# Places of a gathered expert's tokens: spread over the partitions by a matmul out of a resident table, in place of a broadcast transfer

## The reference

```python
scores = jax.nn.sigmoid(xf @ w_router)
_, idx = lax.top_k(jnp.where(expert_mask, biased, NEG_INF_2), TOP_K)
w = jnp.take_along_axis(scores, idx, axis=-1)
w = w / (jnp.sum(w, axis=-1, keepdims=True) + 1e-20) * ROUTED_SCALE
...
out = swiglu_2(xpad[toks], w1[e], w3[e], w2[e])        # for each block of one expert's tokens
return out * wts[:, None].astype(out.dtype)
...
routed = jax.ops.segment_sum(y.reshape(n_slots, D), slot_tok, num_segments=T + 1)[:T]
shared = swiglu_2(xf, ws1, ws3, ws2)
```

## Time and profile before

| | |
|---|---|
| median of three runs | 3819.14 us (3814.4 to 3822.09) |
| the profiled execution | 3815.19 us |
| its span | 3813.2 us, mean granted clock 0.964 |
| TensorE busy | 3526.2 us, 92% |
| VectorE, ScalarE busy | 2335.9 us (61%), 1474.9 us (39%) |
| DMA | 842.63 MB, mean 221 GB/s |
| chain that ended last | TensorE 76%, DMA 10%, VectorE 9%, ScalarE 3% |

### The profile page before, as it was taken

How to read it: one execution, slowest core, us unless ns; L and a number is a source line. 1 busy time by engine, 2 the same in 40 slices (tenths; PEclk the granted TensorE clock), 3 DMA queues, 4 the chain that set the end, 5 groups by cost and what they waited for, 6 DMA issues and landing times.

```text
span 3813.2 us, 52585 instructions
## 1 busy us (share of the span) xinstructions
PE 3526.2 (92%) x21065; PEld 2984.2 (78%) x21065; DVE 2335.9 (61%) x3513; ACT 1474.9 (39%) x2212; POOL 242.0 (6%) x337
## 2 busy tenths in 40 slices
PE   4998899998899997899999999999989999999999
PEld 2997799997699886689777777778878976666676
DVE  6774376775377465446666666656644766666666
ACT  1432234432143203223555555541232355555554
POOL 3010000010001001000000000000000000000000
PEclk9998899998899998889999999999988999999999
DMA  7785176695068645236889998875522688898886
GB/s 250 253 294 191 58 259 223 212 311 177 28 229 302 216 138 192 73 98 214 272 274 297 289 299 283 271 244 193 166 77 83 217 277 270 285 290 278 285 277 193
DMA packets 580320, 842.63 MB, mean 221 GB/s; under 512 B 22715, under 2 KB 489760, under 8 KB 578832
## 3 DMA queue, kind: packets, MB, share of 16 engines
q1 hardware_dynamic: 514508, 665.85, 53.3%
q0 software_dynamic: 41056, 147.35, 11.7%
q10 hardware_dynamic: 24548, 26.57, 2.8%
HBM read 836.37 MB, written 3.33 MB: 220 GB/s over the span
## 4 chain that ended last, share of the span: by engine, by line
PE 76%; DMA 10%; DVE 9%; ACT 3%; issue 2%; SPq 1%; DVEq 0%; POOL 0%; ACTq 0%
PE bank L987 13%; PE bank L892 11%; PE bank L893 11%; PE bank L894 11%; PE bank L1332 8%; DMA ring<-in_w 3%; DMA far_up<-in_w 3%; DMA wmod<-in_w_mod 3%; PE bank L1199 2%; PE bank L1345 2%; PE bank L1302 2%; PE bank L1303 2%; PE bank L1297 2%; PE bank L1299 1%; PE bank L1298 1%
## 5 line engine op out<-in xcount | busy, mean ns | idle before, releaser
L894 PE MATMUL bank<-hh,ring_lo 128*128 128x256 f32 (+1 forms) x2176 | 620.5, 285 | 0.0
L892 PE MATMUL bank<-hh,hi 128*128 128x256 f32 (+1 forms) x1984 | 570.2, 287 | 16.0 <-issue 12.3
L893 PE MATMUL bank<-h_lo,hi 128*128 128x256 f32 (+1 forms) x1984 | 566.4, 286 | 0.0
L987 PE MATMUL bank<-h,ring 128*128 128x256 f32 x2432 | 553.5, 388 | 8.4 <-ACT h L1509 8.4
L987 PEld LDWEIGHTS bank<-h,ring 128*128 128x128 f32 x2432 | 474.8, 196 | 79.5 <-issue 11.8
L894 PEld LDWEIGHTS bank<-hh,ring_lo 128*128 128x128 f32 (+1 forms) x2176 | 418.6, 192 | 0.0
L892 PEld LDWEIGHTS bank<-hh,hi 128*128 128x128 f32 (+1 forms) x1984 | 382.1, 193 | 24.6 <-issue 17.6
L893 PEld LDWEIGHTS bank<-h_lo,hi 128*128 128x128 f32 (+1 forms) x1984 | 382.2, 193 | 0.5 <-issue 0.5
L892 PE MATMUL bank<-hid,hi 128*128 128x256 f32 (+1 forms) x1216 | 348.1, 286 | 0.0
L893 PE MATMUL bank<-hid_lo,hi 128*128 128x256 f32 (+1 forms) x1216 | 345.4, 284 | 0.0
L894 PE MATMUL bank<-hid,ring_lo 128*128 128x256 f32 (+1 forms) x1088 | 308.9, 284 | 0.0
(11 more groups left out here) (372 smaller groups left out, 6615.1 us busy)
## 6 DMA issues: line engine op xcount, KB each, us to landing
ring<-in_w SPq DMA_DIRECT2D x258, 1024.0 KB, 12.7
ring<-in_ffn_w SPq DMA_DIRECT2D x120, 1024.0 KB, 10.6
wmod<-in_w_mod POOLq DMA_DIRECT2D x216, 512.0 KB, 5.6
far_up<-in_w SPq DMA_DIRECT2D x84, 1024.0 KB, 11.8
ring<-in_w_in SPq DMA_DIRECT2D x74, 1024.0 KB, 6.3
work<-in_w SPq DMA_DIRECT2D x42, 1024.0 KB
ring<-in_w_out SPq DMA_DIRECT2D x16, 1024.0 KB, 5.1
ring<-in_w_mod SPq DMA_DIRECT2D x12, 1024.0 KB, 16.5
```

The source lines that it names most:

```text
L892: pe.matmul(o, w_hi, x_hi, start=start, stop=False, skip_group_check=True)
L893: pe.matmul(o, w_hi, x_lo, start=False, stop=False, skip_group_check=True)
L894: return pe.matmul(o, w_lo, x_hi, start=False, stop=stop, skip_group_check=True)
L987: ins = pe.matmul(o[:, half * T:(half + 1) * T], l_, r_, start=(k == 0), stop=(k == KD - 1))
```

## The change

The table of places stays in SBUF (`place_rows`, 64 partitions by 256 tokens, over `pT`), in the rounded type. For each gathered unit one matmul is put behind `turn_few`: its weights are column `rank` of a 64 by 64 unit matrix (`rank_row`), repeated 128 times, so that the product is row `rank` of the table in all 128 partitions, in the free half of bank 1. `few_turned` now counts this matmul. `spread_slots` reads bank 1 in place of the buffers and waits for `few_turned`; ScalarE's `turned_few` waits for `spread_done` as well, and so do TensorE's `turn_few` and the second up projection of a dense unit behind a gathered one, since they write the bank. The table in HBM, its store, the 98 loads and their semaphores go.

```diff
--- before.py
+++ after.py
@@ -104,7 +104,6 @@
     return WIDE if ORDER[n][0] == "wide" else NARROW
 
 
-RANKS = [r for k, r in ORDER if k in ("wide", "narrow")]
 GATHER_NO = {n: sum(k in ("wide", "narrow") for k, _ in ORDER[:n]) for n in range(len(ORDER) + 1)}
 
 
@@ -358,7 +357,8 @@
         product = nc.alloc_sbuf_tensor_at("product", [P, T], F32, offset=place["macc"] + 4 * (2 * D + 3 * T))
         picks = rounded("picks", [P, 4, 4, P], "wmod")
         spread = rounded("spread", [P, 2, T], "axial")
-        places = [work[:, 65, :], std[:, :]]
+        place_rows = rounded("place_rows", [P, T], "pT")
+        rank_row = rounded("rank_row", [P, N_EXPERTS], "work", 65 * T)
 
         glu = tiles(16, CT)
         ya, yc = tiles(0, 4), tiles(20, 4)
@@ -397,7 +397,6 @@
 
         window_dram = nc.dram_tensor("window_scratch", [NQ, 512], F32, kind="Internal")
         gates_dram = nc.dram_tensor("gates_scratch", [DEPTH, N_EXPERTS, T], F32, kind="Internal")
-        places_dram = nc.dram_tensor("places_scratch", [DEPTH, N_EXPERTS, T], F32, kind="Internal")
         rows_dram = [nc.dram_tensor(f"rows_scratch{l}", [1 + T, D], F32, kind="Internal") for l in range(DEPTH)]
 
 
@@ -421,10 +420,9 @@
             sem(n) for n in ("consts_in", "vecs_in", "x_in", "filter_in", "masks_in", "router_in", "gates_out",
                              "window_out", "bias_in"))
         gates_in = [sem(f"gates_in{v}") for v in range(2)]
-        places_in = [sem(f"places_in{v}") for v in range(2)]
         got_in = [sem(f"got_in{v}") for v in range(2)]
-        sort_in, zero_row_in, rows_in, places_out, kz_cleared = (
-            sem(n) for n in ("sort_in", "zero_row_in", "rows_in", "places_out", "kz_cleared"))
+        sort_in, zero_row_in, rows_in, kz_cleared = (
+            sem(n) for n in ("sort_in", "zero_row_in", "rows_in", "kz_cleared"))
         order_ready = sem("order_ready")
         turned_in, hg_hi_done, hg_done = sem("turned_in"), sem("hg_hi_done"), sem("hg_done")
         pre_done, product_done, few_turned = sem("pre_done"), sem("product_done"), sem("few_turned")
@@ -1305,6 +1303,10 @@
 
                 def turn_few(n):
                     p, wide = GATHER_NO[n], ORDER[n][0] == "wide"
+                    if p == 0:
+                        pe.wait_ge(*X("copied", 1))
+                    else:
+                        pe.wait_ge(spread_done, g0 + p)
                     if wide:
                         pe.wait_ge(product_done, g0 + p + 1)
                         for c in range(2):
@@ -1313,7 +1315,10 @@
                         pe.wait_ge(pre_done, g0 + p + 1)
                         for c in range(4):
                             ins = pe.matmul(bank[1][:, c * NARROW:(c + 1) * NARROW], pre[:, c * P:(c + 1) * P], fold, start=True, stop=True)
-                    ins.then_inc(few_turned, 1)
+
+                    rank = ORDER[n][1]
+                    pe.matmul(bank[1][:, T:2 * T], rank_row[0:N_EXPERTS, rank:rank + 1].to_broadcast([N_EXPERTS, P]), place_rows[0:N_EXPERTS, :],
+                              start=True, stop=True).then_inc(few_turned, 1)
 
                 def finish(n, last=False):
                     if not gathers(n):
@@ -1393,6 +1398,8 @@
                             scatter(n - 2)
                         finish(n - 1)
                         sum_slots(X, LISTED.get((n, 0), ()))
+                        if gathers(n - 1):
+                            pe.wait_ge(spread_done, g0 + GATHER_NO[n])
                         up_dense(n, 1)
                         sum_slots(X, LISTED.get((n, 1), ()))
                         turn_rows(n, GATHER_NO[n])
@@ -1773,9 +1780,6 @@
                 def load_gates(rank):
                     act.dma_start(gates[:, rank % 2, :], gates_dram.ap()[l][rank:rank + 1, :].partition_broadcast(P)).then_inc(gates_in[rank % 2], 16)
 
-                def load_places(p):
-                    act.dma_start(places[p % 2], places_dram.ap()[l][RANKS[p]:RANKS[p] + 1, :].partition_broadcast(P)).then_inc(places_in[p % 2], 16)
-
                 def columns_hi(n):
                     if not gathers(n):
                         return
@@ -1810,6 +1814,7 @@
                         act.activation(pre[:, :], bank[0][:, :], ACT.Copy).then_inc(pre_done, 1)
 
                 def turned_few(n):
+                    act.wait_ge(spread_done, g0 + GATHER_NO[n] + 1)
                     act.wait_ge(few_turned, g0 + GATHER_NO[n] + 1)
                     if slots(n) == WIDE:
                         act.activation(hidden_few[:, :], bank[1][:, 0:T], ACT.Copy).then_inc(hid_done, 2)
@@ -1834,9 +1839,6 @@
                         split_ups(n + 1, 1)
                         out_hi(n - 1)
                         turned_few(n)
-                        if 1 <= GATHER_NO[n] < GATHERED - 1:
-                            act.wait_ge(spread_done, g0 + GATHER_NO[n])
-                            load_places(GATHER_NO[n] + 1)
                     else:
                         rank = ORDER[n][1]
                         if 1 <= rank < WIDE_FROM - 1:
@@ -1850,14 +1852,8 @@
                         silu_dense(n, 1)
                         columns_hi(n + 1)
                         split_ups(n + 1, 1)
-                        if n == 2:
-                            act.wait_ge(*X("copied", 1))
-                            act.dma_start(places_dram.ap()[l], pT_flat[0:N_EXPERTS, 0:T]).then_inc(places_out, 16)
                         if n == 3:
-                            act.wait_ge(places_out, 16 * (l + 1))
                             act.wait_ge(rows_in, 16 * TB * (l + 1))
-                            load_places(0)
-                            load_places(1)
 
             setup_loads()
             load_router(0)
@@ -2523,7 +2519,8 @@
 
             def copy_places(X):
                 dve.wait_ge(*X("turned", 1))
-                dve.tensor_copy(pT_flat[0:N_EXPERTS, 0:T], bank[2][0:N_EXPERTS, 0:T]).then_inc(X["copied"], 1)
+                then(dve.tensor_copy(rank_row[0:N_EXPERTS, :], M["ident"][0:N_EXPERTS, 0:N_EXPERTS]))
+                dve.tensor_copy(place_rows[0:N_EXPERTS, :], bank[2][0:N_EXPERTS, 0:T]).then_inc(X["copied"], 1)
 
             def pick_slots(X, batches):
                 for i in batches:
@@ -2607,10 +2604,10 @@
                 def spread_slots(n):
 
                     p = GATHER_NO[n]
-                    dve.wait_ge(places_in[p % 2], nth(l, p, GATHERED))
+                    dve.wait_ge(few_turned, g0 + p + 1)
                     if g0 + p >= 2:
                         dve.wait_ge(scattered, g0 + p - 1)
-                    dve.tensor_scalar(spread[:, p % 2, :], places[p % 2], own if slots(n) == WIDE else own_few, None, ALU.is_equal).then_inc(spread_done, 1)
+                    dve.tensor_scalar(spread[:, p % 2, :], bank[1][:, T:2 * T], own if slots(n) == WIDE else own_few, None, ALU.is_equal).then_inc(spread_done, 1)
 
                 rank_experts(X)
                 hidden_dense(0, 0)
```

## The result

| | before | after |
|---|---|---|
| median of 20 runs each | 3822.14 us | 3827.52 us |
| ratio, 95% interval | | 1.0019 (1.001 to 1.0028) |
| span of the profiled execution | 3813.2 us | 3826.1 us |
| the two expert layers (first gathered up projection to last down projection, by the timelines) | 709.5 + 721.2 us | 719.6 + 717.9 us |
| TensorE's waits at the down projection | 49.0 us in 34 | 27.6 us in 32 |

I had forecast 3812.7 us. By the ratio the change costs 7 us, and the two expert layers of the profiles show it: +6.8 us. The other 6 us between the spans lie outside of them, where the change touches only the making of the table. What lies outside of the layers took 2379 to 2390 us in the fourteen profiles of this document (before 2382, after 2389), whatever the edit.

What follows compares the result with a forecast made beforehand. TensorE was taken to set the pace, with DMA costing time only through its idle gaps. The terms +11.8 - 2.2 + 7.7 - 3.9 - 19.8 = -6.4 us gave 3812.7 us from the median 3819.14, range 3801 to 3829.

Steps and rivals of the forecast that it cites:

- the new matmul (11.8 - 2.2): TensorE, 98 gathered units: 0.12 us each, 11.8 us, less 2.2 us free in 18 units behind dense ones.
- chain in 14 wide-narrow places: Wide unit, then narrow, then another gathered: spread behind the turn makes the columns 0.55 us late, 7.7 us in all.
- waits for late weights, absorption included: TensorE's varying waits at the down projection: 19.8 us gained, and 3.9 us of added costs absorbed in what is left.
- I stay at 0.12: Each new 256-column matmul on TensorE costs 0.12 us, like rounded ones in the trace where TensorE never idles.
- a costly matmul: Rival, chance 0.09: type or single column breaks TensorE's pace, 0.25 us or more each, 12.7 us more, 3825.4 us.
- the upper bound: The new matmul costs at most its whole run from start to end, 0.28 us, 27 us in all.
- The relief: Without the 98 broadcasts weights arrive earlier, so TensorE's waits at the down projection shrink by 19.8 us, bounds 7 and 22.
- The 1.8 us at each long wait: Eight TensorE waits over 1.8 us each shorten by 1.8 us, taken between 1.5 and 2.3, 14.4 us together.
- the own packets: Lower bound of the gain per broadcast: only its own packets' DMA time, 0.5 us, goes.
- The hole of the earlier trace: Around the places' packets the DMA share falls to 0.54 for 2 us, so about 1.0 us of room is lost.
- the first rival: Chance 0.23: weights come in time everywhere, all 24.2 us of waits go, 3812 us, or 3804.5 with the wide-narrow step hidden.
- The rival of a chain in every pair: Chance 0.13: the chain through VectorE costs 0.4 us in 62 gathered units, 25 us instead of 7.7, 3834 or 3829 us.

Runs made afterwards that it cites:

- e1: The changed kernel with table and one-hot column of 128 rows instead of 64, the added rows of the column zeros; ratio 0.9954 to the kernel before.
- e5: The kernel before with places loaded once per buffer of a layer, 4 transfers instead of 98, and no new matmul; ratio 0.9931.
- e6: The kernel before with places spread over 32 partitions instead of 128 for all but the first two experts of a layer; ratio 0.9921.

## Why the forecast was wrong

By its steps, on the two layers:

| term | forecast | measured |
|---|---|---|
| the new matmul (11.8 - 2.2) | +9.6 | +38.3 |
| chain in 14 wide-narrow places | +7.7 | +2.7 (14 x 0.19) |
| waits for late weights, absorption included | -23.7 | -24.9 |
| slow down projections behind long waits | not seen | -10.1 |
| sum | -6.4 | +6.0 (layers: +6.8) |

- **The failing step** is "I stay at 0.12, since table and column are both of the rounded type, as in scatter". The price came from matmuls of 128 or 96 rows, and the new one uses 64 rows of the array between neighbours that use 128. I had named a costly matmul as a rival at 0.09, with a price of 0.25 us and the type or the single column as its reason; the size was too small and the reasons were the wrong ones, as e1 shows by keeping both. That its time, 3825.4 us, lies 1 us from what the ratio makes of 3819.14 us is luck: its matmul was 12.7 us dearer than mine and the measured one 28.7, and the smaller chain, the greater relief and the slow down projections took back 16.3. The price from start to end, 0.28 us, which I called the upper bound, was none either: the steps make the neighbours wait as well.
- **The trace of before had the step in it.** TensorE goes from the up projection to the transposes of the next columns, which have 64 rows for a narrow unit and 128 for a wide one:

```profile
2099.45 0.40 PE L1303 MATMUL bank<-far_up_lo,hg 128*128 128x512 f32 x1
2099.78 0.71 PE L1284 MATMUL bank<-mats,got 64*128 64x64 f32 x8
...
1851.18 0.40 PE L1303 MATMUL bank<-ring_lo,hg 128*128 128x512 f32 x1
1851.41 1.03 PE L1284 MATMUL bank<-mats,got 128*128 128x128 f32 x8
```

  0.33 us to the 64-row ones, 0.23 to the 128-row ones. Leaving them, the next matmul starts 0.152 us behind the last one of 64 rows and 0.028 behind one of 128. Together 0.22 us for a step and back. The two kinds differ in size too, so this is a hint and e1 the proof. Over 80 units it is 18 us, enough to turn the sum of -6.4 positive.
- **Not every step in rows costs.** In the window of the earlier trace rows 48 of the 830 matmuls take 96 rows, and TensorE goes from 128 to 96 and back at its usual 0.12 us, at all 16 such places among these matmuls (L892 to L894) in the trace:

```profile
119.24 0.28 PE L894 MATMUL bank<-hh,ring_lo 128*128 128x256 f32 x1
119.36 0.28 PE L892 MATMUL bank<-hid,hi 96*128 96x256 f32 x1
...
122.12 0.28 PE L894 MATMUL bank<-hid,ring_lo 96*128 96x256 f32 x1
122.24 0.28 PE L892 MATMUL bank<-hh,hi 128*128 128x256 f32 x1
```

- The Trainium skill ("TensorEngine Tiling (Array Packing)", Key Properties) says that changing the tiling mode drains TensorE. The runs fit that, if going from 128 rows to 64 is such a change and going to 96 is not; that the lost time is a drain they do not show. It is 0.33 us a pair behind a narrow turn and 0.39 behind a wide one.
- **The relief** was right in mechanism, and near in size: e5, the relief by itself, takes 21.5 us off the waits where I had 19.8. The 1.8 us at each long wait can't be read from the changed kernel, where no late wait is left, but four of the eight long ones are left in part in e5, shorter by 2.1, 1.4, 2.2 and 1.7 us, in the mean 1.8, and far from the 0.5 of the own packets. The mean hides a spread: another, of 2.77 us, went whole. The hole of the earlier trace rows isn't behind every transfer either; at the next one, 3588 to 3590 us, the DMA share is 1.03. That the weights come in time everywhere was the first rival (0.23), and with the matmul's delay added they do. What I missed is the clock behind the waits. The windows that I had read the earlier trace rows were ones without long waits.
- **The chain** was right, and its 0.55 us a place is 0.57 in e1, the kernel whose matmul costs what I had assumed. In the changed kernel the matmul's excess covers two thirds of it. The rival of a chain in every pair fell: the scatter to down projection of the other pairs is unchanged to 0.01 us.
- Spread out of PSUM takes 0.48 us, not 0.41. I had priced the compare by a copy.
- Had the matmul been of 128 rows, the same change would have given 0.9954, some 3801.6 us on the median before: at the lower edge of the range and not at its middle, by the clock term.

Open: 0.8 us of the layers, and why two of the eight down projections behind long waits, one of them behind the longest, kept their clock. Why a quarter of a broadcast costs nothing. The stretches outside of the layers, which differed by up to 11.5 us between profiles, were not looked into.

## What to carry to other kernels

Price a new matmul by ones that use the same part of the array between the same neighbours. If it stands between matmuls of 128 rows and has 64 itself, fill it up with zero rows, and try the same for columns of weights that fall short: the added rows and columns cost nothing in time here, the steps cost 0.1 to 0.25 us each way. Before such a matmul goes where the code has room for it, look for a wait of the same engine that it can stand in. And when a wait goes, look at the clock behind it: the work after a long one may have run slow, and that comes back too.

## What the hardware showed that I had not expected

- Going from 128 rows of the array to 64 and back costs TensorE 0.33 to 0.39 us around one rounded matmul. Going to 96 rows and back costs nothing.
- A down projection of 64 columns between neighbours of 128 costs 0.09 us ahead of it and 0.1 to 0.25 behind. Not every step in columns does: the first matmul behind the 64-column transposes of L1253 starts 0.028 us behind the last, as it does behind 128-column ones.
- A compare of 128x256 takes 0.48 us out of PSUM and 0.35 out of SBUF.
- A broadcast to 32 partitions in place of 128 costs the weights behind it nothing that can be measured (layers -29.9 us in e6, -30.6 in e5).
